# A mixture-of-experts step on one core: another order of the three kinds of expert pass

## The chip, the cores and the metric

The kernel runs on one core of a Trainium2 chip. The metric is device time in microseconds (us); lower is better. A core has TensorE (PE in the profile; its weight loads are listed as PEld), VectorE (DVE), ScalarE (ACT), GpSimd (POOL) and SyncE (SP). In this kernel SP issues nearly all transfers. Sixteen DMA engines carry them.

## The reference, cut to what matters

One layer of a decoder runs over 256 prompt tokens and 32 sample tokens, 288 tokens together, each 1024 wide. After attention and a state-space part, the last and by far the longest part is a mixture of 32 experts, in which each token uses 4:

```
logits = x2d @ w_router + b_router;  top_v, top_i = top_k(logits, 4);  gates = softmax(top_v)
h   = x_rows @ w_gate_up[e] + b_gate_up[e]              # 1024 -> 2048, for each expert e
act = min(h_even, 7) * sigmoid(1.702 * min(h_even, 7)) * (clip(h_odd, -7, 7) + 1)
out = act @ w_down[e] + b_down[e]                       # 1024 -> 1024
y[token] += gate * out                                  # summed over the token's four experts
```

All weights are float32: 8.4 MB of `w_gate_up` and 4.2 MB of `w_down` for each expert, 403 MB for all 32.

## The kernel before, in words

**Attention, state-space part and router** take up to about 190 us. The router counts how many tokens each expert has and sorts the experts by that count. Experts 0 and 1 always stand at positions 0 and 1.

**Kinds.** The experts run one after another at positions p = 0 to 31 (passes). `KINDS` gives each position one of three kinds. A narrow pass ("few") has room for 32 tokens, a medium pass ("mid") for 64, and a many-slot pass ("many") for 96: it does the work of a medium and of a narrow pass side by side. The sorted list fills the kinds: the fullest experts get the "many" positions, the next ones "mid", the emptiest "few" (`rank_at`, lines 1795 to 1803). There are 4 many, 14 mid and 14 few. Tokens that still don't fit would run in further passes behind position 31; this input has none.

**One pass on PE** (`expert`, line 1014): gate_up in eight chunks, one for every 128 of the 1024 input rows; the results of the pass before are combined in the middle of it (gates after chunk 1, `combine` after chunk 4). Then the hidden values are turned, the next pass's tokens are gathered and turned (`gather` for a wide pass, `gather_s` for a narrow one, both if the next is many), and `down` multiplies with `w_down`. ACT and DVE copy, clamp and gate between these steps, and DVE adds each pass's result to the output (`accumulate`, line 1925).

**Weights.** `gu_ring` has four slots of 2 MB, together one expert's `w_gate_up`. `dn_ring` has four, together two experts' `w_down`, in two halves each. SP (`load_others`, line 369) issues in the order dn(p), gu(p), dn(p+1), gu(p+1) and waits before each: gu(p) slot k waits until pass p-1 has used chunks 2k and 2k+1 (`gu_used`), and dn(p) half h waits until pass p-2 has used that half (`dn_used`). For the last pair the order is dn(30), gu(30), gu(31), dn(31). An expert is thus six transfers of 2 MB. All go through one queue in order.

**Loops.** On PE and ACT positions 0 and 1 are written out, positions 2 to 17 are a hardware loop of four rounds (`BODY`), positions 18 to 29 a loop of two rounds of six (`LATE`), and 30 and 31 are written out. On DVE only the four rounds are a loop; from position 18 on all is written out, with a few small operations between the passes that list the leftover tokens (`item_order`, `item_pass`).

Of the kernel before, what the change touches and what calls it, by code (L numbers as in the profile page):

```python
# [35 lines left out]
NE, TOPK = 32, 4  # L36
# [5 lines left out]
ITEMS = T * TOPK // SLOTS  # L42
PAIRS = NE // 2
GU_SLOTS = 4
GU_ROWS = KT // GU_SLOTS
FEW = 32
BODY, ROUNDS = ("few", "many", "few", "mid"), 4
LATE, LATER = ("few", "mid", "mid") * 2, 2
FIRST_LATE = 2 + len(BODY) * ROUNDS
KINDS = ["mid"] * 2 + list(BODY) * ROUNDS + list(LATE) * LATER + ["few"] * 2  # L50
ITEM_PART = 6
WIDE = [sum(k != "few" for k in KINDS[:p]) for p in range(NE + 1)]
SLIM = [sum(k != "mid" for k in KINDS[:p]) for p in range(NE + 1)]
# [24 lines left out]
def build(nc, a):  # L78
# [439 lines left out]
    def _(pe):  # L518
# [495 lines left out]
        def expert(p, w, s, kind, before, after, j, fill):  # L1014

            w_before, s_before = w - (before != "few"), s - (before != "mid")
            w_after, s_after = w + (kind != "few"), s + (kind != "mid")
            gate_up(p, w, s, kind, range(0, 2))
            if before == "bias":
                turn_gates(0)  # L1020
            else:
                if before == "many":
                    pe.wait_ge(S("ye_s_ready"), s_before + 1)
                if before != "few":
                    turn_gates(w)
                if before != "mid":
                    turn_gates_s(s_before)
            gate_up(p, w, s, kind, range(2, 5))
            if before == "bias":
                gate_bias()  # L1030
            else:
                combine(p, w_before, s_before, before)
            gate_up(p, w, s, kind, range(5, 8))
            pe.wait_ge(S("acc_done"), p * 4 + 4)
            if kind != "few":
                turn_hidden(w)
            if kind != "mid":
                turn_hidden_s(s)
            if after in ("mid", "many"):
                gather(w_after)  # L1040
            if after in ("few", "many"):
                gather_s(s_after)
            if after in ("mid", "many"):
                turn_gathered(w_after)
            if after in ("few", "many"):
                turn_gathered_s(s_after)
            if after is None:
                turn_gates_s(s)
            down(w, s, kind, after, s_after, j, fill)
# [4 lines left out]
        busy(0, xg[:, 0, 0:2 * P], 1)  # L1054
        expert(0, 0, 0, KINDS[0], "bias", KINDS[1], 0, 1)
        expert(1, 1, 0, KINDS[1], KINDS[0], KINDS[2], 1, 1)
        with pe.Fori(0, ROUNDS) as i:
            for k in range(4):
                expert(i * 4 + (2 + k), i * (WIDE[6] - WIDE[2]) + WIDE[2 + k], i * (SLIM[6] - SLIM[2]) + SLIM[2 + k],
                       BODY[k], BODY[k - 1], BODY[(k + 1) % 4], k % 2, i * 2 + (k // 2 + 2))  # L1060
        with pe.Fori(0, LATER) as i:
            for k in range(6):
                p = FIRST_LATE + k
                expert(i * 6 + p, i * (WIDE[p + 6] - WIDE[p]) + WIDE[p], i * (SLIM[p + 6] - SLIM[p]) + SLIM[p],
                       KINDS[p], KINDS[p - 1], KINDS[p + 1], k % 2, i * 3 + (p // 2 + 1))
        expert(NE - 2, N_WIDE, N_SLIM - 2, "few", "mid", "few", 0, PAIRS)
        expert(NE - 1, N_WIDE, N_SLIM - 1, "few", "few", None, 1, PAIRS)
        combine(NE, N_WIDE, N_SLIM - 1, "few")

        pe.wait_ge(S("list_ready"), 1)  # L1070
# [19 lines left out]
    def _(act):  # L1090
# [287 lines left out]
        def act_expert(p, w, s, kind, before, after):  # L1378

            w_after, s_after = w + (kind != "few"), s + (kind != "mid")  # L1380
            if before == "bias":
                act_gates(0)
            else:
                if before != "few":
                    act_gates(w)
                if before != "mid":
                    act_gates_s(s - 1)
            if kind != "few":
                act_gate(w)
# [12 lines left out]
            if after in ("mid", "many"):  # L1402
                act_turned(w_after)
            if after in ("few", "many"):
                act_turned_s(s_after)
            if after is None:
                act_gates_s(s)
            if kind != "few":
                act_result(p)
            if kind != "mid":  # L1410
                act_result_s(p)
# [2 lines left out]
        act_turned(0)  # L1414
        act_expert(0, 0, 0, KINDS[0], "bias", KINDS[1])
        act_expert(1, 1, 0, KINDS[1], KINDS[0], KINDS[2])
        with act.Fori(0, ROUNDS) as i:
            for k in range(4):
                act_expert(i * 4 + (2 + k), i * (WIDE[6] - WIDE[2]) + WIDE[2 + k], i * (SLIM[6] - SLIM[2]) + SLIM[2 + k],
                           BODY[k], BODY[k - 1], BODY[(k + 1) % 4])  # L1420
        with act.Fori(0, LATER) as i:
            for k in range(6):
                p = FIRST_LATE + k
                act_expert(i * 6 + p, i * (WIDE[p + 6] - WIDE[p]) + WIDE[p], i * (SLIM[p + 6] - SLIM[p]) + SLIM[p],
                           KINDS[p], KINDS[p - 1], KINDS[p + 1])
        act_expert(NE - 2, N_WIDE, N_SLIM - 2, "few", "mid", "few")
        act_expert(NE - 1, N_WIDE, N_SLIM - 1, "few", "few", None)

        act.wait_ge(S("list_ready"), 1)
        n = act.alloc_register("act_items")  # L1430
# [14 lines left out]
    def _(dve):  # L1445
        X = nc.vector
# [485 lines left out]
        def slots_of(c):  # L1932

            return pos[M, :, bass.ds(c, 1)]
# [55 lines left out]
        def expert_at(k, p):  # L1990
            dve.reg_load(regs[k], ord_e[0:1, p:p + 1] if isinstance(p, int) else ord_e[0:1, bass.ds(p, 1)])
            return dve.snap(regs[k], min_val=0, max_val=NE - 1)

        def expert(p, w, s, kind, before, after, x):

            x_before, x_now, x_after = x
            w_after, s_after = w + (kind != "few"), s + (kind != "mid")
            if before != "bias":
                if before != "few":
                    gated(slots_of(x_before), bass.ds(x_before, 1), w)  # L2000
                if before != "mid":
# [11 lines left out]
        dve.wait_ge(S("order_ready"), 1)  # L2013
        expert(0, 0, 0, KINDS[0], "bias", KINDS[1], (0, 0, 1))
        expert(1, 1, 0, KINDS[1], KINDS[0], KINDS[2], (0, 1, expert_at(0, 2)))
        with dve.Fori(0, ROUNDS) as i:
            x = [expert_at(k, i * 4 + (1 + k)) for k in range(6)]
            for k in range(4):
                expert(i * 4 + (2 + k), i * (WIDE[6] - WIDE[2]) + WIDE[2 + k], i * (SLIM[6] - SLIM[2]) + SLIM[2 + k],
                       BODY[k], BODY[k - 1], BODY[(k + 1) % 4], x[k:k + 3])  # L2020

        def expert_alone(p):
            expert(p, WIDE[p], SLIM[p], KINDS[p], KINDS[p - 1], KINDS[p + 1], [expert_at(k, p - 1 + k) for k in range(3)])

        expert_alone(18)
        expert_alone(19)
        item_order()
        for p in range(20, 26):
            expert_alone(p)
            item_pass(p - 20)  # L2030
        X.tensor_copy(list_e[:, 0:ITEMS + 1], list_f[:, 0:ITEMS + 1]).then_inc(S("list_ready"), 1)
        for p in range(26, NE - 1):
            expert_alone(p)

        n = dve.alloc_register("dve_items")
        x_reg = dve.alloc_register("dve_expert")
        y_reg = dve.alloc_register("dve_next")
        dve.wait_ge(S("list_ready"), 1)
        x_before, x_last = expert_at(0, NE - 2), expert_at(1, NE - 1)
        gated_s(slots_of(x_before), 0, bass.ds(x_before, 1))  # L2040
        accumulate(NE - 1)
        gated_s(slots_of(x_last), 0, bass.ds(x_last, 1))
        hidden_s(N_SLIM - 1, N_WIDE + N_SLIM - 1, x_last)
# [155 lines left out]
```

## Time and profile before

| | before |
|---|---|
| median of 3 runs | 1131.55 us (1131.29 to 1132.45) |
| profiled execution | 1130.87 us |
| its span | 1128.6 us |
| mean granted TensorE clock | 0.971 |
| PE busy | 987.5 us, 88% |
| DVE busy, ACT busy | 397.1 us, 35%; 205.1 us, 18% |
| bytes read from HBM | 419.86 MB |
| DMA over the span | 378 GB/s |

The times of all rows below count from the start of the span; 2.3 us of the profiled execution lie outside it. A matmul's end is modelled, and matmuls overlap a little, so where a step ends is best read from the start of the next one. An expert's pass is found in the rows by the tiles: `gu_ring,xe` is gate_up of a medium pass, `gu_ring,xe_s` of a narrow one, and `dn_ring,hT` and `dn_ring,hT_s` are their `down`. Where both tiles alternate, it is a many pass.

### The profile page before, as it was taken

Reading aid. Unit: us, or ns where it says so; the run is one execution under the profiler, and the core shown is the slowest. Engines: PE = TensorE matmul, PEld = TensorE weight load, DVE = VectorE, ACT = ScalarE, POOL = GpSimd, SP = SyncE. Lnnn points to the kernel's source line nnn. Section 1 sums busy time; section 2 is a strip of 40 time slices with the busy share of each in tenths; the row PEclk is TensorE's granted clock in tenths of the full one; section 3 lists DMA queues with packets and bytes.
Section 4 is the critical chain, followed back from the end, with each engine's and each line's share of the span. In section 5 each row is a group of like instructions: output and inputs, shape, how many; then the busy total and the mean of one; then the engine's idle time right before and its main releaser. Section 6 shows DMA issues by size and latency. Waiting matters only on the chain.

```text
span 1128.6 us, 16526 instructions
## 1 busy us (share of the span) xinstructions
PE 987.5 (88%) x6588; PEld 425.3 (38%) x6588; DVE 397.1 (35%) x898; ACT 205.1 (18%) x441; POOL 7.0 (1%) x7
## 2 busy tenths in 40 slices
PE   6987999999988898889988998979879878969985
PEld 5765875333233323322333233323333323323331
DVE  6978646222322222221323122313333333222223
ACT  4676333111111111110111111111111111111110
POOL 1000000000000000000000000000000000000000
PEclk9967999999999999999999999999999999999998
DMA  9513872899999999999999999999999999999995
GB/s 359 173 48 98 329 309 82 349 428 427 393 408 424 426 428 405 431 425 427 408 427 427 427 406 428 427 427 427 428 427 427 425 429 428 427 427 427 428 427 235
DMA packets 39149, 426.27 MB, mean 378 GB/s; under 512 B 7045, under 2 KB 10245, under 8 KB 12705
## 3 DMA queue, kind: packets, MB, share of 16 engines
q1 hardware_dynamic: 37296, 422.87, 89.6%
q10 hardware_dynamic: 1728, 2.11, 0.5%
q8 instruction: 63, 1.03, 0.4%
q0 software_dynamic: 48, 0.15, 0.0%
q14 instruction: 14, 0.11, 0.0%
HBM read 419.86 MB, written 2.51 MB: 374 GB/s over the span
## 4 chain that ended last, share of the span: by engine, by line
PE 70%; DMA 17%; DVE 6%; issue 3%; ACT 3%; ACTq 1%; DVEq 0%; SPq 0%
PE banks L520 66%; DMA gu_ring<-w_gu_dram 14%; DVE xT L1929 2%; DMA dn_ring<-w_dn_dram 2%; PE banks L906 1%; DVE raw L1883 1%; PE banks L862 1%; DVE hl L1895 1%; DVE hT L1900 1%; ACT gath L1323 1%; PE banks L960 1%; ACT x_tok L1312 1%; PE banks L913 1%; ACT s_p L1224 0%; PE banks L656 0%
## 5 line engine op out<-in xcount | busy, mean ns | idle before, releaser
L520 PE MATMUL banks<-gu_ring,xe 128*64 128x512 f32 x1152 | 269.8, 610 | 16.5 <-DMA gu_ring<-w_gu_dram 16.2
L1929 DVE TENSOR_TENSOR xT<-xT,banks 128x576 f32<-128x576 f32 x132 | 93.8, 751 | 491.8 <-PE banks L520 491.7
L520 PE MATMUL banks<-gu_ring,xe_s 128*32 128x512 f32 x1152 | 143.0, 608 | 22.7 <-issue 11.5
L520 PEld LDWEIGHTS banks<-gu_ring,xe 128*64 128x64 f32 x1152 | 77.7, 139 | 178.2 <-issue 153.8
L520 PE MATMUL banks<-dn_ring,hT 128*64 128x512 f32 x576 | 129.3, 597 | 4.9 <-DVE hT L1900 4.9
L520 PE MATMUL banks<-dn_ring,hT_s 128*32 128x256 f32 x1152 | 70.3, 392 | 5.6 <-ACT xe_s L1357 3.2
L520 PEld LDWEIGHTS banks<-gu_ring,xe_s 128*32 128x32 f32 x1152 | 29.8, 110 | 109.4 <-issue 87.1
L520 PEld LDWEIGHTS banks<-dn_ring,hT 128*64 128x64 f32 x576 | 39.2, 137 | 79.4 <-issue 73.0
L520 PE MATMUL banks<-gT,ye 64*128 64x288 f32 x288 | 48.9, 454 | 10.9 <-DVE xT L1929 10.9
L1338 ACT ACTIVATE raw<-banks 128x512 f32<-128x512 f32 x18 | 10.8, 597 | 248.7 <-PE banks L520 248.7
L520 PEld LDWEIGHTS banks<-dn_ring,hT_s 128*32 128x32 f32 x1152 | 35.7, 112 | 40.2 <-issue 17.1
L520 PE MATMUL banks<-x_tok,oh 96*64 96x512 f32 x216 | 50.3, 601 | 0.0
L520 PE MATMUL banks<-gT_s,ye_s 32*128 32x288 f32 x288 | 27.6, 453 | 21.7 <-DVE xT L1929 21.1
L1883 DVE COPY raw<-banks 128x512 f32<-128x512 f32 x18 | 12.4, 692 | 87.3 <-PE banks L520 87.3
L520 PEld LDWEIGHTS banks<-gT,ye 64*128 64x128 f32 x288 | 24.5, 192 | 42.6 <-DVE xT L1929 24.5
L520 PE MATMUL banks<-xg,w_in 128*128 128x288 f32 x160 | 39.8, 406 | 0.0
L1367 ACT ACTIVATE raw_s<-banks 128x512 f32<-128x512 f32 x18 | 10.8, 597 | 144.5 <-PE banks L520 144.5
L1347 ACT ACTIVATE ye<-banks 128x512 f32<-128x512 f32 x18 | 10.8, 597 | 135.9 <-PE banks L520 135.9
L520 PEld LDWEIGHTS banks<-xg,w_in 128*128 128x128 f32 x160 | 30.4, 190 | 8.4
L520 PE MATMUL banks<-aT,w_out 128*128 128x288 f32 x128 | 32.3, 409 | 1.0 <-ACT aT L1263 1.0
L906 PE MATMUL banks<-ident,raw 128*128 128x128 f32 x144 | 26.8, 309 | 2.2
L906 PEld LDWEIGHTS banks<-ident,raw 128*128 128x128 f32 x144 | 20.0, 208 | 20.3 <-issue 14.7
(347 smaller groups left out, 864.6 us busy)
## 6 DMA issues: line engine op xcount, KB each, us to landing
gu_ring<-w_gu_dram SPq DMA_DIRECT2D x120, 2048.0 KB, 19.9
dn_ring<-w_dn_dram SPq DMA_DIRECT2D x64, 2048.0 KB, 18.0
gu_ring<-w_gu_dram SPq DMA_DIRECT2D x16, 1024.0 KB, 8.3
w_out<-w_out_dram SPq DMA_DIRECT2D x2, 2048.0 KB, 10.0
w_in<-w_in_dram SPq DMA_DIRECT2D x3, 1024.0 KB, 16.3
w_in<-w_in_dram SPq DMA_DIRECT2D x4, 512.0 KB, 9.9
W<-W1c SPq DMA_DIRECT2D x16, 128.0 KB, 2.3
w_glu<-w_glu_dram SPq DMA_DIRECT2D x1, 2048.0 KB, 8.6
```

Of the source, the lines that this page charges most:

```text
L520: return nc.tensor.matmul(out, lhsT, rhs, start=start, stop=stop, **kw)
L862: last = pe.transpose(pb[6][:, c * P:(c + 1) * P], gath[:, c * P:(c + 1) * P], ident[:])
L906: last = pe.transpose(pb[2 + part][:, c * P:(c + 1) * P], hidden_cols(raw[:, part], c), ident[:])
L913: last = pe.transpose(pb[0][:, c * P:(c + 1) * P], hidden_cols(raw_s[:], c), ident[:])
L960: last = pe.transpose(pb[7][:, t * MT:(t + 1) * MT], goh[0:MT, t], ident[0:MT, 0:MT])
L1312: A(half.rearrange("p (s i f) -> p s f i", i=GU_ROWS, f=P), pb[XB[u]][0:MT, :].rearrange("p (s f i) -> p s f i", i=GU_ROWS, f=P), ACT.Copy ...
L1323: A(gath[:], pb[5][:], ACT.Copy).then_inc(S("gath_ready"), 1)
L1338: A(blocks_out(raw[:, 0]), blocks_in(pb[0]), ACT.Copy).then_inc(S("g_copied"), 1)
L1883: X.tensor_copy(blocks_out(raw[:, 1]), blocks_in(pb[1])).then_inc(S("l_copied"), 1)
L1895: X.scalar_tensor_tensor(out=hl[:], in0=hl[:], scalar=1.0, in1=hg[:], op0=ALU.add, op1=ALU.mult).then_inc(S("h_step"), 1)
L1900: X.scalar_tensor_tensor(out=hT[:], in0=th[:], scalar=1.0, in1=hl[:], op0=ALU.add, op1=ALU.mult).then_inc(S("h_ready"), 1)
L1929: X.tensor_tensor(two, two, pair[(1, 3)[n % 2]].rearrange("p (h f) -> p h f", h=2)[:, :, 0:T], ALU.add).then_inc(S("acc_done"), 1)
```

## The change

The order of kinds is another. The number of each kind stays the same.

```
position   0 1 | 2 ...                                              31
before     M M | f X f M  f X f M  f X f M  f X f M | f M M f M M f M M f M M | f f
after      M M f | f X M f  f X M f  f X M f  f X M f | f M M f M M f M M f M M | f
           M = medium, f = narrow (few), X = many-slot
```

So each round of four becomes narrow, many, medium, narrow, and starts one position later. The last four positions were medium, medium, narrow, narrow and become narrow, medium, medium, narrow. On PE and ACT the late part is no longer a loop. The order in which SP issues the loads is untouched.

```diff
-BODY, ROUNDS = ("few", "many", "few", "mid"), 4
-LATE, LATER = ("few", "mid", "mid") * 2, 2
-FIRST_LATE = 2 + len(BODY) * ROUNDS
-KINDS = ["mid"] * 2 + list(BODY) * ROUNDS + list(LATE) * LATER + ["few"] * 2
+BODY, ROUNDS = ("few", "many", "mid", "few"), 4
+FIRST_ROUND = 3
+FIRST_LATE = FIRST_ROUND + len(BODY) * ROUNDS
+KINDS = ["mid"] * 2 + ["few"] + list(BODY) * ROUNDS + ["few", "mid", "mid"] * 4 + ["few"]
...
+        def expert_alone(p):
+            expert(p, WIDE[p], SLIM[p], KINDS[p], KINDS[p - 1], KINDS[p + 1] if p + 1 < NE else None, p % 2, p // 2 + 1)
+
+        expert_alone(2)
         with pe.Fori(0, ROUNDS) as i:
             for k in range(4):
-                expert(i * 4 + (2 + k), i * (WIDE[6] - WIDE[2]) + WIDE[2 + k], i * (SLIM[6] - SLIM[2]) + SLIM[2 + k],
-                       BODY[k], BODY[k - 1], BODY[(k + 1) % 4], k % 2, i * 2 + (k // 2 + 2))
-        with pe.Fori(0, LATER) as i:
-            for k in range(6):
-                p = FIRST_LATE + k
...
+                p = FIRST_ROUND + k
+                expert(i * 4 + p, i * (WIDE[7] - WIDE[3]) + WIDE[p], i * (SLIM[7] - SLIM[3]) + SLIM[p],
+                       BODY[k], BODY[k - 1], BODY[(k + 1) % 4], p % 2, i * 2 + (p // 2 + 1))
+        for p in range(FIRST_LATE, NE):
+            expert_alone(p)
         combine(NE, N_WIDE, N_SLIM - 1, "few")
```

ACT is changed in the same way. DVE's loop moves by one position too, `item_order` stands behind position 20 instead of 19, the six `item_pass` behind 21 to 26 instead of 20 to 25, and at the end DVE prepares the gates of a medium pass 30 (`gated`) instead of a narrow one (`gated_s`). `rank_at` is written in pieces of evenly spaced positions: the narrow positions took three pieces and now take six, the others as many as before.

## Rows read from the trace of the kernel before

**Rows 1.** Windows: us; busy of PE, PEld, DVE, ACT, POOL; PEclk, DMA share, GB/s

```profile
225.00:680.00 455.00, 408.13 (x3093) 145.67 (x3091) 117.84 (x260) 53.53 (x115) 0.00 (x0) 1.00 0.99 420
680.00:1110.00 430.00, 368.36 (x2356) 134.03 (x2357) 129.27 (x254) 46.32 (x91) 0.00 (x0) 0.98 1.01 427
```

**Rows 2.** Chain that ended last, at its end: start, us, what

```profile
1090.54 26.09 DMA dn_ring<-w_dn_dram
...
1116.66 2.81 PE banks L520 x32
```

**Rows 3.** Timeline of PE, positions 7 to 10: start, us, engine, line, operation

```profile
391.12 1.94 PE L520 MATMUL banks<-gu_ring,xe 128*64 128x512 f32 x8
...
419.43 1.50 PE L520 MATMUL banks<-x_tok,oh_s 96*32 96x256 f32 x24
...
422.05 3.65 PE L520 MATMUL banks<-dn_ring,hT 128*64 128x512 f32 x16 [0.17 <-DVE hT L1900]
...
433.12 1.90 PE L520 MATMUL banks<-gu_ring,xe_s 128*32 128x512 f32 x16
...
447.86 2.79 PE L520 MATMUL banks<-x_tok,oh 96*64 96x512 f32 x12
...
451.94 3.66 PE L520 MATMUL banks<-dn_ring,hT_s 128*32 128x256 f32 x64
455.53 3.65 PE L520 MATMUL banks<-gu_ring,xe 128*64 128x512 f32 x16
...
477.84 7.09 PE L520 MATMUL banks<-dn_ring,hT 128*64 128x512 f32 x32 [0.41 <-DVE hT L1900]
487.06 1.92 PE L520 MATMUL banks<-gu_ring,xe_s 128*32 128x512 f32 x16 [2.13 <-issue]
```

**Rows 4.** Timeline of SP's queue: issues of w_down for positions 9, 11, 13

```profile
429.77 4.06 SPq L343 DMA_DIRECT2D dn_ring<-w_dn_dram  x2
481.67 3.76 SPq L343 DMA_DIRECT2D dn_ring<-w_dn_dram  x2
549.00 4.06 SPq L343 DMA_DIRECT2D dn_ring<-w_dn_dram  x2
```

**Rows 5.** Issue to landing: gu(4) slot 0 (277.6), dn(5) (310.2), dn(19) (720.1)

```profile
DMA to landing us min/median/max: 18.0/18.0/18.0
...
DMA to landing us min/median/max: 7.8/7.8/7.8
...
DMA to landing us min/median/max: 16.6/16.6/16.6
```

**Rows 6.** Timeline of PE, positions 18 and 29 to 31

```profile
723.33 1.92 PE L520 MATMUL banks<-gu_ring,xe_s 128*32 128x512 f32 x16
...
739.51 3.66 PE L520 MATMUL banks<-dn_ring,hT_s 128*32 128x256 f32 x64
...
1046.53 3.60 PE L520 MATMUL banks<-gu_ring,xe 128*64 128x512 f32 x16
...
1075.73 1.92 PE L520 MATMUL banks<-gu_ring,xe_s 128*32 128x512 f32 x16
...
1082.46 1.07 PE L520 MATMUL banks<-gu_ring,xe_s 128*32 128x512 f32 x8 [2.55 <-DMA gu_ring<-w_gu_dram]
...
1093.65 3.66 PE L520 MATMUL banks<-dn_ring,hT_s 128*32 128x256 f32 x64 [0.47 <-ACT xe_s L1357]
...
1097.12 1.90 PE L520 MATMUL banks<-gu_ring,xe_s 128*32 128x512 f32 x16
...
1102.12 1.07 PE L520 MATMUL banks<-gu_ring,xe_s 128*32 128x512 f32 x8 [0.84 <-DMA gu_ring<-w_gu_dram]
...
1112.75 3.64 PE L520 MATMUL banks<-dn_ring,hT_s 128*32 128x256 f32 x32 [2.11 <-DVE hT_s L1922]
```

**Rows 7.** Timeline of DVE: the copies that write rank_at

```profile
161.08 0.71 DVE L1801 COPY place<-iota 128x4 f32<-128x4 f32 x9
```

More of the change, by code:

```diff
@@ L1056, in _ @@
         expert(1, 1, 0, KINDS[1], KINDS[0], KINDS[2], 1, 1)
+        def expert_alone(p):
+            expert(p, WIDE[p], SLIM[p], KINDS[p], KINDS[p - 1], KINDS[p + 1] if p + 1 < NE else None, p % 2, p // 2 + 1)
+        expert_alone(2)
         with pe.Fori(0, ROUNDS) as i:
             for k in range(4):
-                expert(i * 4 + (2 + k), i * (WIDE[6] - WIDE[2]) + WIDE[2 + k], i * (SLIM[6] - SLIM[2]) + SLIM[2 + k],
-                       BODY[k], BODY[k - 1], BODY[(k + 1) % 4], k % 2, i * 2 + (k // 2 + 2))
-        with pe.Fori(0, LATER) as i:
-            for k in range(6):
-                p = FIRST_LATE + k
[L1064 to L1067, printed above, removed]
+                p = FIRST_ROUND + k
[3 more added lines that the diff above has]
+            expert_alone(p)
         combine(NE, N_WIDE, N_SLIM - 1, "few")
@@ L1416, in _, with act_expert_alone @@
         act_expert(1, 1, 0, KINDS[1], KINDS[0], KINDS[2])
+        def act_expert_alone(p):
+            act_expert(p, WIDE[p], SLIM[p], KINDS[p], KINDS[p - 1], KINDS[p + 1] if p + 1 < NE else None)
+        act_expert_alone(2)
         with act.Fori(0, ROUNDS) as i:
             for k in range(4):
-                act_expert(i * 4 + (2 + k), i * (WIDE[6] - WIDE[2]) + WIDE[2 + k], i * (SLIM[6] - SLIM[2]) + SLIM[2 + k],
+                p = FIRST_ROUND + k
+                act_expert(i * 4 + p, i * (WIDE[7] - WIDE[3]) + WIDE[p], i * (SLIM[7] - SLIM[3]) + SLIM[p],
                            BODY[k], BODY[k - 1], BODY[(k + 1) % 4])
[L1421 to L1427, printed above, removed]
+        for p in range(FIRST_LATE, NE):
+            act_expert_alone(p)
         act.wait_ge(S("list_ready"), 1)
@@ L2015, in _ @@
         expert(1, 1, 0, KINDS[1], KINDS[0], KINDS[2], (0, 1, expert_at(0, 2)))
[L2016 to L2020, printed above, removed]
         def expert_alone(p):
             expert(p, WIDE[p], SLIM[p], KINDS[p], KINDS[p - 1], KINDS[p + 1], [expert_at(k, p - 1 + k) for k in range(3)])
[L2025 to L2028, printed above, removed]
-            expert_alone(p)
[L2030 to L2033, printed above, removed]
+        expert_alone(2)
+        with dve.Fori(0, ROUNDS) as i:
+            x = [expert_at(k, i * 4 + (2 + k)) for k in range(6)]
+            for k in range(4):
+                p = FIRST_ROUND + k
+                expert(i * 4 + p, i * (WIDE[7] - WIDE[3]) + WIDE[p], i * (SLIM[7] - SLIM[3]) + SLIM[p],
+                       BODY[k], BODY[k - 1], BODY[(k + 1) % 4], x[k:k + 3])
+        for p in range(FIRST_LATE, NE - 1):
+            expert_alone(p)
+            if p == FIRST_LATE + 1:
+                item_order()
+            if FIRST_LATE + 1 < p < FIRST_LATE + 8:
+                item_pass(p - (FIRST_LATE + 2))
+            if p == FIRST_LATE + 7:
+                X.tensor_copy(list_e[:, 0:ITEMS + 1], list_f[:, 0:ITEMS + 1]).then_inc(S("list_ready"), 1)
         n = dve.alloc_register("dve_items")
@@ L2039, in _ @@
         x_before, x_last = expert_at(0, NE - 2), expert_at(1, NE - 1)
-        gated_s(slots_of(x_before), 0, bass.ds(x_before, 1))
+        gated(slots_of(x_before), bass.ds(x_before, 1), N_WIDE)
         accumulate(NE - 1)
```

## The prediction

> **What bounds the kernel now.** I read the rate of the transfers first, then the chain, then the timelines of PE and SP. From 680 to 1110 us the DMA engines move 427 GB/s with no gap (DMA share 1.01), while PE is busy for 368 of 430 us [rows 1]. A transfer of 2 MB (2097152 bytes) takes 4.9 us at that rate, and an expert, six of them, 29.5 us. So the late part is bound by the weights, and PE waits for them (2.55 us and 0.84 us in the last two passes) [rows 6]. From 225 to 680 us the rate is 420 GB/s [rows 1]: 455 us times 7/427 is 7.5 us in which the DMA engines had nothing to do. In that stretch PE is the longer one. Each round of four begins 119.2 us after the one before (549.00 - 429.77) [rows 4], against 4 x 29.5 = 118. At the end the chain waits 26.09 us for the last half of `w_down` and goes on with PE at 1116.66 [rows 2]. A change of order moves no byte. It can change three things: the DMA engines' idle time in the rounds, PE's time for a round, and what PE still has to do once the last weights have landed.
>
> **Lengths of the pieces of a pass, from [rows 3, 6].** "Front" is from the start of gate_up to the start of `down`.
> - Many, next narrow: front 422.05 - 391.12 = 30.9, `down` 433.12 - 422.05 = 11.1. The first half of `w_down` is released 429.77 - 422.05 = 7.7 after `down` began [rows 3, 4].
> - Narrow after many, next medium: front 451.94 - 433.12 = 18.8, `down` 3.6.
> - Narrow after medium, next medium: front 739.51 - 723.33 = 16.2. So to combine a many pass costs 2.6 more than a medium one.
> - Narrow after medium, next narrow: front 1093.65 - 1075.73, less the wait of 2.55, = 15.4, 0.8 shorter because less is gathered.
> - Medium after narrow: front 477.84 - 455.53 = 22.3, `down` 7.1, its first half released after 3.8 (481.67) [rows 3, 4].
> - The loop's back edge: 2.1 us of "issue" before 487.06. From there to the next many pass it is 391.12 + 119.2 - 487.06 = 23.3, which holds whatever the edge costs later.
>
> **Part 1, the many pass is followed by a medium one.** This pair is not in the trace. The medium pass's gather takes 2.79 us against 1.50 for the narrow one [rows 3], and in a many pass nothing is left that hides it. The front becomes longer by between 0 (all hidden behind DVE) and 2.8 (the whole gather late). I take the difference of the gathers, 1.3: front 32.2. The medium pass behind it has to combine the many pass: 22.3 + 2.6 = 24.9. With M the start of the many pass, the medium one starts at M + 32.2 + 11.1 = M + 43.3, its `down` at M + 68.2, and it releases its half of `w_down` at M + 72.0. A transfer issued into an empty queue lands 7.8 us later [rows 5], so at M + 79.8. If the queue never ran dry, this transfer, the 16th after the slot that started M, would land at M + 16 x 4.9 = M + 78.4. The queue therefore still runs dry for 1.4 us in each round, but behind the medium pass instead of within the many pass (its own release at M + 39.9 would land at M + 47.7, and 10 transfers take until M + 49.0). The Trainium skill, page "DMA: Bandwidth & Descriptors", section "Anatomy of one DMA", gives a fixed cost of about 2.0 us for a transfer beside its bytes. This trace shows 7.8 - 4.9 = 2.9 on a transfer of SP's queue, and the measured one stands. By 2.0 the sum would be lower by 0.9.
>
> **Part 2, PE's time for a round.** M + 68.2 + 7.1 (medium `down`) + 15.4 + 3.6 (narrow, next narrow) + 2.1 (edge) + 23.3 = M + 119.7. By the transfers it is 79.8 + 8 x 4.9 = M + 119.0. The two nearly coincide (4.9 us for each transfer is the bare rate), whereas before PE alone decided with a margin. Paths so close end a little after the later one, and I take 120.0, 0.8 more than before.
>
> **Part 3, the first round.** Positions 2 and 3 are both narrow now, so PE is at the first many pass early and waits for its weights: gu(4) slot 0 was issued at 277.6 and landed 18.0 later, at 295.6 [rows 5]. The fourth many pass then starts at 295.6 + 3 x 120.0 = 655.6. The transfer that follows the medium pass behind it is dn(19), which lands at 655.6 + 79.8 = 735.4; before it landed at 720.1 + 16.6 = 736.7 [rows 5]. From there to the end both orders are bound by the same 77 transfers. All that the new rounds do to the stream of weights is -1.3 us. The idle time that goes with the first many pass comes back as four small gaps and a slower round.
>
> **Part 4, the loop that goes.** The late part's back edge lies where PE waits for weights anyway (2.55 us in a late narrow pass [rows 6]). It is worth 0, and 2.1 if that cover were missing. The page "Runtime: NRT & Kernel Launch" of the Trainium skill, section "Instruction fetch mechanics", says that a taken branch breaks the sequential prefetch and that kernels therefore prefer unrolling. The 2.13 us at the edge agree. By that rule alone the change would give 2.1 us.
>
> **Part 5, the end.** Before, the last passes were medium, narrow, narrow, and PE was waiting when the last `w_down` landed. Now they are medium, medium, narrow. The second medium pass of a pair started at 1046.53 as position 29 [rows 6] and is now position 30, one expert of weights later: 1076.0. A medium pass after a medium one, next narrow, took 1075.73 - 1046.53 = 29.2 without a wait, so the last pass starts at 1105.2. Its front, 1112.75 - 1097.12 less the wait of 0.84 = 14.8, and a `down` of 3.6 end at 1123.6. The last weights still land at 1116.6. The gain of part 3 moves both ends alike. Before, `down` ended at 1116.66 + 2.81 = 1119.5 [rows 2]. PE now has the later end, by 4.1 us. What follows is the same: one narrow combine, four additions, the output. What would shorten this is only an earlier start of that medium pass, and its weights forbid it.
>
> **Part 6, three more small copies** for `rank_at`, nine in 0.71 us [rows 7], ahead of work on which the router waits: +0.2.
>
> **Sum:** 0.2 - 1.3 + 0 + 4.1 = +3.0. The profiled execution of 1130.87 (span 1128.6 and 2.3 around it) would be 1133.9. The median of the runs is 0.7 above that execution, so I predict 1134.6. The lower bound of part 1's front (0 instead of 1.3) takes 1.3 from each of three rounds and from the last release, 5.2 together, and makes the sum -2.2 or 1129.4. The upper one (2.8) adds 1.5 x 4 = 6.0 and makes it +9.0 or 1140.6. I stay near the middle, since the row of the gather is the nearest one.
>
> **Rivals.**
> - A, the end is covered: the last narrow pass finds its hidden values ready, the extra 4.1 does not appear and 0.2 - 1.3 = -1.1 is left: 1130.5. For it: DVE and ACT have slack. Against it: all of the 14.8 + 3.6 is PE's own chain with one wait for DVE. Chance 0.2.
> - B, the other side (against my forecast of slower): the rounds never let the queue run dry. Two narrow passes in a row give PE a lead just before the many pass, and if the medium pass's release comes before M + 70 the 7.5 us of idle time all go. Then 7.5 of the stream is won: 0.2 - 7.5 + 4.1 = -3.2, 1128.3. This needs a front shorter by 2 us than worked out and a PE round below 118. It decides from the point where the round falls under 118 us. Chance 0.13.
> - C, both late paths give way: the medium pass behind the many one releases 1.2 us later still (its gather waits for ACT, or PE's clock falls while it waits for weights before the many pass), and since no margin is left each of the four rounds carries it: 4 x 1.2 = 4.8 more, 1139.4. For it: before, PE had room to absorb such a thing, now both paths are critical. Chance 0.2.
> - My forecast: 0.47.
>
> The change does what it says: no token passes from one kind to another, as the counts of kinds are equal.
>
> **Numbers.** A measurement of this kernel tells 0.2%, 2.3 us, from no change: below 1129.3 is faster, above 1133.8 slower. Faster holds B, 0.13. Slower holds C and most of my forecast, which stands only 0.8 above the bound: 0.2 + 0.39 = 0.59. The rest, 0.28, is no change. The range reaches from 1129.5 (the lower bound, and A with a little from the stream) to 1139.5 (C). My case alone would be 1132.5 to 1137.
>
> **What would show it.** In the profile of the changed kernel: (1) the rate from 305 to 315 us near 427 GB/s, with dips near 365 to 375 and once a round after; (2) a period of 119.5 to 120.5 us; (3) many passes that start when their weights land, the first at about 295.6; (4) the last half of `w_down` landed near 1115 while PE is still in gate_up or before `down` of the last pass, which ends near 1122; (5) the chain at the end on PE, not on the DMA of `dn_ring`. If the last `down` still waits for `dn_ring`, part 5 is wrong. If the rate shows no dips in the rounds, part 1 is. If the period is over 121, C is right.

## The result, and the profile after

The changed kernel takes 1137.79 us (median of 15 runs, 1132.75 to 1144.24), the kernel before 1132.31 us (15 runs on the same chip, 1129.29 to 1135.46): a ratio of 1.0048, 95% interval 1.0034 to 1.0062. It is slower, by 5.5 us where 3.0 was predicted. On another chip the same kernel took 1136.54 us (12 runs) against 1133.64, 1.0023 [0.9999, 1.0046], an interval that just reaches no loss. So the loss is some 2.6 to 5.5 us. The profiled execution of the changed kernel took 1139.23 us, with a span of 1137.3 and a mean granted clock of 0.964.

The windows, which answer to [rows 1] (us; busy of PE, PEld, DVE, ACT, POOL; PEclk, DMA share, GB/s); the narrow ones are the idle times within a round:

```profile
225.00:680.00 455.00, 403.52 (x3043) 143.20 (x3045) 114.34 (x252) 51.69 (x111) 0.00 (x0) 0.97 0.99 417
305.00:315.00 10.00, 8.49 (x56) 2.35 (x54) 2.56 (x4) 0.00 (x0) 0.00 (x0) 0.96 1.02 433
365.00:380.00 15.00, 14.00 (x87) 4.78 (x89) 3.06 (x8) 1.55 (x4) 0.00 (x0) 1.00 0.94 376
485.00:500.00 15.00, 13.84 (x93) 4.48 (x85) 3.03 (x9) 2.29 (x5) 0.00 (x0) 1.00 0.93 371
680.00:1110.00 430.00, 374.10 (x2347) 135.82 (x2340) 128.85 (x254) 47.28 (x93) 0.00 (x0) 0.97 1.00 426
```

The one window of these where the kernel before had its gap:

```profile
305.00:315.00 10.00, 10.00 (x102) 3.40 (x98) 1.24 (x5) 0.87 (x2) 0.00 (x0) 1.00 0.70 262
```

The large gap in the first many pass is gone (262 before, 433 after). Gaps have come behind the medium pass: 376 and 371 instead of 427 over 15 us, some 2 us of idle time in each round. And a smaller one is left in the many pass, at its own release of `w_down`, which now comes later (337.82, 458.67 and 581.22 in the first three rounds, 310.22 in the first before). The largest of these:

```profile
570.00:585.00 15.00, 14.30 (x114) 4.88 (x112) 5.53 (x17) 2.43 (x5) 0.00 (x0) 1.00 0.89 355
```

That is 2.5 us of idle time. Over the whole stretch the rate is no better (417 against 420), and the late part is the same.

PE's timeline through two rounds, which answers to [rows 3]:

```profile
296.07 1.94 PE L520 MATMUL banks<-gu_ring,xe 128*64 128x512 f32 x8 [0.49 <-DMA gu_ring<-w_gu_dram]
...
330.10 3.65 PE L520 MATMUL banks<-dn_ring,hT 128*64 128x512 f32 x16
...
341.28 3.65 PE L520 MATMUL banks<-gu_ring,xe 128*64 128x512 f32 x16
...
366.07 7.09 PE L520 MATMUL banks<-dn_ring,hT 128*64 128x512 f32 x32 [0.42 <-DVE hT L1900]
373.08 1.92 PE L520 MATMUL banks<-gu_ring,xe_s 128*32 128x512 f32 x16
...
388.25 3.66 PE L520 MATMUL banks<-dn_ring,hT_s 128*32 128x256 f32 x64 [0.55 <-ACT xe_s L1357]
391.72 1.91 PE L520 MATMUL banks<-gu_ring,xe_s 128*32 128x512 f32 x16
...
398.47 1.07 PE L520 MATMUL banks<-gu_ring,xe_s 128*32 128x512 f32 x8 [2.60 <-DMA gu_ring<-w_gu_dram]
...
418.55 1.94 PE L520 MATMUL banks<-gu_ring,xe 128*64 128x512 f32 x8
...
450.94 3.65 PE L520 MATMUL banks<-dn_ring,hT 128*64 128x512 f32 x16
...
541.10 1.94 PE L520 MATMUL banks<-gu_ring,xe 128*64 128x512 f32 x8
660.14 1.94 PE L520 MATMUL banks<-gu_ring,xe 128*64 128x512 f32 x8 [1.86 <-DMA gu_ring<-w_gu_dram]
```

SP's releases by the medium pass, once a round (they answer to [rows 4]):

```profile
369.90 3.76 SPq L343 DMA_DIRECT2D dn_ring<-w_dn_dram  x2
490.75 3.76 SPq L343 DMA_DIRECT2D dn_ring<-w_dn_dram  x2
613.29 3.76 SPq L343 DMA_DIRECT2D dn_ring<-w_dn_dram  x2
732.33 3.76 SPq L343 DMA_DIRECT2D dn_ring<-w_dn_dram  x2
```

Issue to landing of the first transfer of the first and fourth of these, and of the last two transfers of all (issued from 1097.0 to 1097.5), as in [rows 5]:

```profile
DMA to landing us min/median/max: 9.0/9.0/9.0
...
DMA to landing us min/median/max: 7.6/7.6/7.6
...
DMA to landing us min/median/max: 17.7/19.9/22.1
```

So the last weights are there at 1097.5 + 22.1 = 1119.6, 3.0 later than before. PE's last two passes, which answer to [rows 6], are not waiting for them:

```profile
1078.76 3.60 PE L520 MATMUL banks<-gu_ring,xe 128*64 128x512 f32 x16
...
1107.97 1.92 PE L520 MATMUL banks<-gu_ring,xe_s 128*32 128x512 f32 x16
...
1122.57 5.35 PE L520 MATMUL banks<-dn_ring,hT_s 128*32 128x256 f32 x64 [2.11 <-DVE hT_s L1922]
```

And the end of the chain (start, us, what) is PE's from well before that landing, where it was the transfer's in [rows 2]:

```profile
1089.60 6.74 PE banks L520 x32
...
1100.95 8.94 PE banks L520 x48
...
1110.29 3.42 PE banks L520 x28
...
1114.55 4.18 PE banks L520 x32
```

The span is 8.7 us longer than before (1137.3 - 1128.6): 3.0 because the last weights land later, 5.7 because the span ends 17.7 us after them instead of 12.0. The first part moves from one execution to the next (in the profile on the other chip they landed at 1115.2), the second does not (17.6 there).

### The profile page after: what moved, and what is told of

Read it like the earlier page. It is cut to its first block, busy times and chain, and to the rows that moved or that the text cites. A ratio compares the mean times of both kernels' runs of the same rounds, so it can differ in the third digit from the quotient of the medians.

```text
span 1137.3 us, 16455 instructions
## 1 busy us (share of the span) xinstructions
PE 995.4 (88%) x6588; PEld 426.0 (37%) x6588; DVE 396.7 (35%) x901; ACT 205.2 (18%) x441; POOL 7.0 (1%) x7
## 3 DMA queue, kind: packets, MB, share of 16 engines
q10 hardware_dynamic: 1728, 2.11, 0.5%
## 4 chain that ended last, share of the span: by engine, by line
PE 68%; DMA 19%; DVE 7%; ACT 3%; issue 2%; ACTq 1%; DVEq 0%; SPq 0%
PE banks L520 65%; DMA gu_ring<-w_gu_dram 19%; DVE xT L1929 2%; PE banks L906 1%; DVE raw L1883 1%; PE banks L862 1%; PE banks L960 1%; ACT gath L1323 1%; ACT x_tok L1312 1%; ACT s_p L1224 0%; DVE hl L1895 0%; DVE hT L1900 0%; PE banks L913 0%; PE banks L656 0%; PE banks L967 0%
## 5 line engine op out<-in xcount | busy, mean ns | idle before, releaser
L520 PE MATMUL banks<-gu_ring,xe 128*64 128x512 f32 x1152 | 275.1, 620 | 20.8 <-DMA gu_ring<-w_gu_dram 20.6
L520 PE MATMUL banks<-gu_ring,xe_s 128*32 128x512 f32 x1152 | 146.0, 618 | 17.1 <-DMA gu_ring<-w_gu_dram 17.0
L520 PE MATMUL banks<-gT_s,ye_s 32*128 32x288 f32 x288 | 30.5, 496 | 21.7 <-DVE xT L1929 21.1
L520 PEld LDWEIGHTS banks<-gT_s,ye_s 32*128 32x128 f32 x288 | 12.3, 200 | 45.2 <-DVE xT L1929 28.6
```

What stands on the lines that cost most here:

```text
L520: return nc.tensor.matmul(out, lhsT, rhs, start=start, stop=stop, **kw)
```

## The experiments

M is medium, f narrow, X many-slot. Times are medians in us, each beside the kernel before on the same chip.

| kernel | order | time (range, runs) | before | ratio [95%] |
|---|---|---|---|---|
| changed | MMf (fXMf)x4 (fMM)x4 f | 1137.79 (1132.75-1144.24, 15) | 1132.31 | 1.0048 [1.0034, 1.0062] |
| after_again | the same | 1136.54 (1131.8-1143.3, 12) | 1133.64 | 1.0023 [0.9999, 1.0046] |
| end_back | MMf (fXMf)x4 (fMM)x3 MMff | 1132.99 (1127.27-1137.12, 12) | 1133.28 | 0.9997 [0.998, 1.0013] |
| end_alone | MM (fXfM)x4 (fMM)x3 ffMMf | 1138.73 (1134.86-1143.62, 11) | 1133.28 | 1.0046 [1.0031, 1.0061] |
| unrolled | as before | 1131.55 (1129.99-1136.49, 12) | 1133.28 | 0.9987 [0.9971, 1.0002] |
| body_back | MMf (fXfM)x4 (fMM)x4 f | 1129.1 (1126.87-1130.32, 7) | 1133.28 | 0.9959 [0.9944, 0.9974] |
| no_loop | as before | 1127.91 (1126.08-1130.52, 6) | 1133.79 | 0.9952 [0.9935, 0.997] |
| both_back | MMf (fXfM)x4 (fMM)x3 MMff | 1124.12 (1123.76-1125.09, 5) | 1133.79 | 0.9917 [0.9903, 0.9931] |
| both_no_loop | the same | 1125.12 (1123.49-1125.36, 5) | 1133.79 | 0.9921 [0.9906, 0.9935] |
| end_warm | as changed | 1136.69 (1132.21-1141.53, 12) | 1133.79 | 1.0026 [1.0009, 1.0043] |
| rounds_warm | as changed | 1137.24 (1132.36-1140.74, 12) | 1133.64 | 1.0029 [1.0009, 1.005] |
| both_warm | as changed | 1134.2 (1131.68-1140.45, 12) | 1133.64 | 1.0012 [0.9992, 1.0032] |
| mid_first | MMf (fMXf)x4 (fMM)x4 f | 1134.81 (1131.93-1140.17, 12) | 1133.64 | 1.0007 [0.9988, 1.0026] |

### The end: put back, and made alone

**end_back**: the changed kernel with before's last four kinds. (Of each experiment only the lines that matter are shown. Here DVE also prepares the gates of pass 30 with `gated_s` again, as that pass is narrow.)

```diff
-KINDS = ["mid"] * 2 + ["few"] + list(BODY) * ROUNDS + ["few", "mid", "mid"] * 4 + ["few"]
+KINDS = ["mid"] * 2 + ["few"] + list(BODY) * ROUNDS + ["few", "mid", "mid"] * 3 + ["mid", "mid", "few", "few"]
```

> The changed kernel's rounds with an end of two narrow passes: positions 28 to 31 are medium, medium, narrow, narrow instead of narrow, medium, medium, narrow. Theory 'end' (a medium pass at position 30 leaves PE 4 to 5.5 us of work behind the last weights): this is 4 to 5.5 us faster than the changed kernel (1137.8), so 1132.3 to 1133.8, within 1.5 us of the kernel before. Theory 'rounds' (the medium pass behind each many pass and the clock that falls while PE waits before it cost the time): it keeps the loss, 1136 to 1138. In the profile, by 'end', the last down waits for dn_ring again and ends about 3 us after the last landing instead of 8.

**end_alone**: before's rounds, at before's positions, with a narrow pass last behind two medium ones.

```diff
-BODY, ROUNDS = ("few", "many", "mid", "few"), 4
-FIRST_ROUND = 3
+BODY, ROUNDS = ("few", "many", "few", "mid"), 4
+FIRST_ROUND = 2
-KINDS = ["mid"] * 2 + ["few"] + list(BODY) * ROUNDS + ["few", "mid", "mid"] * 4 + ["few"]
+KINDS = ["mid"] * 2 + list(BODY) * ROUNDS + ["few", "mid", "mid"] * 3 + ["few", "few", "mid", "mid", "few"]
```

> The rounds of the kernel before with the new end: positions 27 to 31 are narrow, narrow, medium, medium, narrow instead of narrow, medium, medium, narrow, narrow; the late part is written out. Theory 'end': 4 to 5.5 us slower than the kernel before (1132.3), 1136.3 to 1137.8. Theory 'rounds': no difference, 1132.

Measured: 0.9997 and 1.0046. With before's end the changed kernel is as fast as before. With the new end alone the kernel before loses 5.2 us. end_alone also has the late part written out, as the changed kernel has. Against unrolled (below), the kernel before with just that, it loses more, 6.7 us by the two ratios (1.0046 and 0.9987). The chain's end of end_back is that of [rows 2] again, the wait for `w_down` and then PE:

```profile
1090.02 26.15 DMA dn_ring<-w_dn_dram
...
1116.22 1.98 PE banks L520 x32
```

The whole measured loss is thus the end's (part 5), and rival A is refuted. The new rounds give nothing and cost nothing that can be measured (end_back is also 1.1 us above unrolled by the ratios, within their intervals).

### The loop edges

**unrolled**: before's order, with positions 18 to 31 written out on PE and ACT as in the changed kernel. **no_loop**: before's order, everything from position 2 written out, on DVE too. In outline, PE's part:

```diff
 # unrolled
+        with pe.Fori(0, ROUNDS) as i:      # positions 2 to 17, before's BODY
+        for p in range(FIRST_LATE, NE):    # instead of before's loop over LATE
+            expert_alone(p)
 # no_loop
-        with pe.Fori(0, ROUNDS) as i:
-            for k in range(4):
-                ...
-        for p in range(FIRST_LATE, NE):
+        for p in range(2, NE):
             expert_alone(p)
```

> The order of the kernel before, with only the late part on PE and ACT written out instead of a loop of two rounds of six. Both main theories: no difference (within 0.5 us), because PE waits for weights in that part. Rival 'fetch' (a taken branch stalls the engine and the written-out form wins that back): 2 us faster. Rival 'fetch the other way' (more code has to be brought in and the transfers share the queues): 1 to 2 us slower, which would be part of the change's loss.

> The order of the kernel before, with all passes from position 2 written out on PE, ACT and DVE, so that no loop edge is left. If the edge (2.1 us of issue and 1.5 more a few chunks later, three times in the rounds) holds up PE where PE is the longer one: a period of 119.2 falls to the transfers' 118, so about 1.2 x 3 = 3.6 us faster, 1129; the first gap of the many pass stays. Rival 'no edge cost' (code has to be brought in either way): 1132 to 1133. Writing out the late part alone gave 1131.6 against 1133.3.

Writing out the late part gives 1.5 us, with an interval from a gain of 3.3 to a loss of 0.2: it excludes neither the 0 of part 4 nor the 2.1 of its rule. All edges together give 5.4 us (interval 3.4 to 7.4). PE's timeline of no_loop shows that the 2.13 us of "issue" behind the medium pass [rows 3] are gone, 358.54 + 7.09 and on at once:

```profile
358.54 7.09 PE L517 MATMUL banks<-dn_ring,hT 128*64 128x512 f32 x32 [0.49 <-DVE hT L1885]
365.56 1.92 PE L517 MATMUL banks<-gu_ring,xe_s 128*32 128x512 f32 x16
```

In the rounds before, where PE was the longer path, the edge did cost time: the releases by the many pass (310.53, 428.63, 545.84, 664.80) come 118.1 us apart on average, which is the 4 x 29.5 of the transfers, where they were 119.2 apart before. The first gap stays (262 GB/s from 305 to 315 us). Its chain at the end shows the last weights 3 us earlier than in [rows 2]:

```profile
1087.47 26.11 DMA dn_ring<-w_dn_dram
...
1113.62 1.98 PE banks L517 x32
```

### The rounds: the same shift, without the many-medium pair

**body_back**: the changed kernel with before's order within a round (narrow, many, narrow, medium), still one position later. Its loop covers positions 7 to 18 in three rounds, and the first round is written out, on all three engines. So it has one edge fewer than the kernel before, beside the late part's.

```diff
-BODY, ROUNDS = ("few", "many", "mid", "few"), 4
-FIRST_ROUND = 3
+BODY, ROUNDS = ("few", "many", "few", "mid"), 3
+FIRST_ROUND = 7
-KINDS = ["mid"] * 2 + ["few"] + list(BODY) * ROUNDS + ["few", "mid", "mid"] * 4 + ["few"]
+KINDS = ["mid"] * 2 + ["few"] + list(BODY) * (ROUNDS + 1) + ["few", "mid", "mid"] * 4 + ["few"]
```

> The changed kernel with a narrow pass between the many and the medium pass again (order after position 2: narrow, many, narrow, medium, four times), the early narrow pass at position 2 and the new end kept. The loop on PE, ACT and DVE covers positions 7 to 18, three rounds instead of four, so one back edge fewer. Theory 'end' alone: equal to the changed kernel less what the stalls behind the medium passes cost, which my arithmetic puts at 5 to 6 us: 1130 to 1132.5, because the start of two narrow passes takes away the long gap of the first many pass. Theory 'rounds are neutral': 1137. In the profile the issue-to-landing gap at the medium pass's release is gone and the many passes start 2 to 5 us after their weights landed.

Measured 1129.1, 0.9959, although it still has the slow end. The window from 225 to 680 us and the end of its chain:

```profile
225.00:680.00 455.00, 408.57 (x3083) 143.94 (x3077) 115.02 (x252) 52.10 (x112) 0.00 (x0) 0.98 1.01 427
```

```profile
1113.05 5.39 PE banks L520 x64
```

The rate is 427, against 417 to 420 in both the kernel before and the changed one: here the queue hardly runs dry. Against the kernel before two things differ in the rounds, the narrow pass more ahead of the first many pass and the fewer loop edges, and this run does not separate them. That the narrow pass is a gain by itself is shown by no_loop and both_no_loop (below), which have no loop at all. Against the changed kernel, whose edges show no cost (part 2 below), what body_back gives back is the price of the medium pass right behind the many one. The chain still ends on PE, in the whole of the last `down` (x64) at the lower clock.

**mid_first**: the heavy pair turned round, medium before many.

```diff
-BODY, ROUNDS = ("few", "many", "mid", "few"), 4
+BODY, ROUNDS = ("few", "mid", "many", "few"), 4
```

> The changed kernel with the body narrow, medium, many, narrow instead of narrow, many, medium, narrow: the medium pass stands before the many pass. Theory 'two heavy passes in a row' (what costs is that PE falls behind the weights by two passes without a narrow one between, and the second of them releases w_down late): the same as the changed kernel within 1.5 us, 1136 to 1139, with the gap now behind the many pass. Rival 'the combine of the many pass in a medium pass' (its longer gates and combine, 2.6 us, are what makes the release late): most of the 9 to 10 us that a narrow pass behind the many pass gave back is won here too, 1129 to 1131.

Measured 1134.81, which is 1.7 below after_again on the same chip and not to be told from it. It lies between the two ranges of its expectation, below the 1136 to 1139 of 'two heavy passes' and well above the 1129 to 1131 of its rival. The queue now runs dry behind the many pass:

```profile
490.00:505.00 15.00, 15.00 (x146) 5.47 (x142) 0.63 (x3) 1.58 (x4) 0.00 (x0) 1.00 0.85 340
```

Its ratio of 1.0007 [0.9988, 1.0026] is apart from body_back's 0.9959 [0.9944, 0.9974]. So what costs is mainly that two heavy passes stand side by side, whichever is first.

### Both parts taken back: the faster kernel

**both_back**: body_back with before's last four kinds. It is the order of before with one narrow pass moved from position 27 to position 2, the late part and the first round written out. **both_no_loop**: the same order, all written out.

```diff
-KINDS = ["mid"] * 2 + ["few"] + list(BODY) * ROUNDS + ["few", "mid", "mid"] * 4 + ["few"]
+KINDS = ["mid"] * 2 + ["few"] + list(BODY) * (ROUNDS + 1) + ["few", "mid", "mid"] * 3 + ["mid", "mid", "few", "few"]
```

> Medium, medium, narrow, then narrow, many, narrow, medium four times, then narrow, medium, medium three times, medium, medium, narrow, narrow. Only the second narrow pass at position 2 and 3 is left of the change. If the end's cost and the rounds' cost are separate terms that add, this is the kernel with a narrow pass behind each many pass (1129.1) less the 5.4 us that the new end cost: 1123.5 to 1124.5, 8 to 9 us faster than the kernel before. Theory 'transfers only' (the earlier start only moves the idle time, and the end hides it): 1129. In the profile the last w_down lands near 1110 and the last down ends 2 to 3 us later.

> The order of the run before this one in name ('both back'), with all passes from position 2 written out. If that order already keeps the transfers without a gap, the loop edges are covered and this gives nothing more: the same time within 1 us, near 1124. If edges still cost, 2 to 3 us less, 1121.

Measured 1124.12, 9.4 us below the kernel before, and 1125.12. Two windows and the end of the chain of both_back:

```profile
225.00:680.00 455.00, 406.65 (x3105) 145.06 (x3105) 117.25 (x256) 52.70 (x113) 0.00 (x0) 0.99 1.01 427
680.00:1105.00 425.00, 370.10 (x2363) 135.41 (x2351) 132.10 (x264) 47.81 (x95) 0.00 (x0) 0.98 1.01 427
```

```profile
1083.76 25.43 DMA dn_ring<-w_dn_dram
...
1109.24 3.69 PE banks L520 x32
```

The stream runs at one rate from 225 us to its end, and the last weights are on the chain 7.4 us earlier than in [rows 2]. The end counts here as it does in end_back: body_back to both_back is 0.9959 to 0.9917, 4.8 us. Writing out the loops that are left adds nothing, as the edges lie beside a stream that is the bound everywhere.

How much of the 9.4 us is the order's? both_no_loop and no_loop, on the same chip, have no loop in either and differ only in where the one narrow pass stands: 1125.12 (1123.49 to 1125.36) against 1127.91 (1126.08 to 1130.52), 2.8 us, or 3.5 by the ratios. Writing out everything in before's order gives 5.4. The move alone, with before's loops kept, was not run. It may be worth more than 3.5 there, since it also covers the edges that are left.

### The clock

In the changed kernel PE waits for weights in the narrow pass ahead of a many one, and its granted clock is low there (windows as above):

```profile
395.00:410.00 15.00, 10.16 (x67) 3.00 (x58) 3.50 (x6) 0.60 (x1) 0.00 (x0) 0.77 1.01 430
515.00:530.00 15.00, 10.51 (x64) 2.47 (x64) 2.84 (x4) 0.32 (x1) 0.00 (x0) 0.66 1.00 428
```

The kernel before had 1.00 from 395 to 410. Three kernels keep PE at work with products whose result nobody reads. **end_warm** puts them ahead of the last `down`, **rounds_warm** into each narrow pass before a many one, **both_warm** does both.

```diff
 # rounds_warm, in expert
+            if kind == "few" and after == "many":
+                gate_up(p, w, s, kind, range(2, 4))
+                busy(1, ident[:], 10)
+                gate_up(p, w, s, kind, range(4, 5))
+            else:
                 gate_up(p, w, s, kind, range(2, 5))
 # end_warm, behind the turning of the last pass's gates
+                busy(1, ident[:], 10)
```

> The changed kernel with ten further matmuls of 128 columns (their result is used by nothing) on PE while it waits for the hidden values of the last pass, just before its down. In the changed kernel's profile that down took 5.35 us against 3.66 for the same work at the full clock. If the wait of 2.1 us is what let the clock fall there: 1 to 1.7 us faster than the changed kernel, 1136 to 1137, down back at 3.7 us. Rival (the clock fell for what lay further back, as the wait for weights at the many passes does): no change, and down stays above 5 us in the profile.

> The changed kernel with ten further matmuls of 128 columns (used by nothing) on PE in each narrow pass that stands before a many pass, at the point where it waits 2.6 to 3 us for the third slot of gu_ring. In the changed kernel's profile the clock falls there (399 to 407 us, 519 to 530 us), the narrow pass and once the many pass become 2 to 3.3 us longer, and the period of the rounds is 120.9, 122.5 and 119.0 us. Theory 'clock' (that fall costs the rounds their time, because behind it nothing is in reserve): periods near 119.3, 3 to 5 us faster than the changed kernel (1137.8), so 1133 to 1135, and a smaller spread than its 11 us. Rival 'release' (the late release of w_down behind the medium pass sets the pace whatever the clock does): 0 to 1 us, 1137.

> The changed kernel with both sets of further matmuls, in the narrow pass before each many pass and before the last down. If the clock's two places are separate terms: 5 to 7 us faster than the changed kernel, 1131 to 1133, which would be what the order itself costs without the clock, about the time of the kernel before. Rival: no more than the better of the two alone, 1135.

PE at the end of end_warm, the filler and the last `down`:

```profile
1119.44 2.42 PE L520 MATMUL banks<-ident 128*128 128x128 f32 x20
1121.79 3.66 PE L520 MATMUL banks<-dn_ring,hT_s 128*32 128x256 f32 x64
```

The `down` is back at 3.66 us, 1.7 shorter than the 5.35 of the changed kernel, where PE had stood idle for 2.11 us ahead of it. The granted clock was 1.00 from 1121 to 1126 us here, and 0.66 from 1122 to 1125.5 in the changed kernel. That piece of the tail is the clock's. But the filler isn't needed for it, and the wait alone does not decide it. These are the same `down` in rounds_warm (no filler at the end), in end_alone, and its first half in both_no_loop:

```profile
1122.88 3.66 PE L520 MATMUL banks<-dn_ring,hT_s 128*32 128x256 f32 x64 [2.10 <-DVE hT_s L1927]
```

```profile
1125.63 6.59 PE L520 MATMUL banks<-dn_ring,hT_s 128*32 128x256 f32 x64 [2.11 <-DVE hT_s L1920]
```

```profile
1107.04 1.93 PE L517 MATMUL banks<-dn_ring,hT_s 128*32 128x256 f32 x32 [2.26 <-DVE hT_s L1907]
```

Behind the same wait the 64 products take 3.66, 5.35 or 6.59 us. From the start of this `down` to the end of the span it is 13.0 us in rounds_warm and end_warm, 14.7 in the changed kernel and 15.8 in end_alone, so the profiles do show the time. end_warm, with one profile, doesn't show that its filler held the clock. What decides it was not tried. The ratios differ by less than their intervals (1.0026 against 1.0048 and 1.0023), so the runs' times don't show the 1.7.

The same places in rounds_warm (windows 5 us longer), with the clock held:

```profile
395.00:415.00 20.00, 17.25 (x149) 7.19 (x141) 5.88 (x14) 3.35 (x8) 0.00 (x0) 1.00 1.01 431
515.00:535.00 20.00, 17.77 (x175) 7.69 (x163) 7.12 (x19) 2.40 (x5) 0.00 (x0) 1.00 1.01 430
```

Here PE waits for weights at the start of the last three many passes (1.85, 0.97 and 0.84 us). In the changed kernel's profile it waits, of these three, only at the fourth, and the third starts late, behind a narrow pass at the lower clock. The periods are 121.9, 119.2 and 119.0 us, against 120.9, 122.5 and 119.0 there and 121.5, 119.1 and 119.1 in after_again. Two of the three are thus near the 119.3 of the theory 'clock'. But its time is no better than that of after_again (1.0029 against 1.0023), and its transfer behind the fourth medium pass is issued at 732.72, as late as in the changed kernel (732.33). So the lower clock in the rounds can cost one execution a little and is not what makes the runs long.

both_warm gave 1134.2, 1.0012 [0.9992, 1.0032]: 2.3 below after_again, which the intervals don't separate, and above the 1131 to 1133 of two terms that add.

**after_again**: the changed kernel once more, beside the last kernels.

> The changed kernel once more, beside the others on the same chip: 1137 to 1138, 5 to 5.5 us slower than the kernel before, with a spread of 8 to 11 us between its executions.

Measured 1136.54, a loss of 2.6 us by the ratio, half of the 5 to 5.5 expected. Its last `down` takes the same 5.35 us:

```profile
1118.13 5.35 PE L520 MATMUL banks<-dn_ring,hT_s 128*32 128x256 f32 x64 [2.10 <-DVE hT_s L1922]
```

## Why the prediction was right, and where it was not

The sign, the place and the mechanism were right: the change loses at the end, on PE, and the rounds give nearly nothing. The measured 1137.79 lies 3.2 above the predicted 1134.6, inside the range, near its slow end. The two profiles show both cases that were named: 1134.87 lies in my own case (1132.5 to 1137), 1139.23 beside rival C's 1139.4. Point by point, with the sum's own terms:

- **Part 1, many then medium: right in the main.** Front of the many pass 450.94 - 418.55 = 32.4 (predicted 32.2; the first one, at 34.0, was longer, with eight products in it that took 3.32 us instead of 1.94). Medium front 366.07 - 341.28 = 24.8 (24.9), its release 3.8 after `down` began. The gap appeared behind the medium pass as worked out. It did not only move, though: one of up to 2.5 us was left in the many pass, since the first many pass had the longer front and the second and third started later than their weights landed (part 2). The size behind the medium pass was a little low: two of the four transfers landed 9.0 and 9.5 us after issue instead of 7.8, two 7.6, so the gap is between 1.2 (1.4 - 0.2) and 3.1 us (1.4 + 1.7).
- **Part 2, PE's round: its edge did not appear.** The sum had 2.1 of "issue" between the two narrow passes and 1.5 more within its 23.3. In the trace `down` at 388.25 + 3.66 is followed by gate_up at 391.72, and instead PE waits for weights 2.60 us later. The edge's cost was read from a medium-narrow pair, and behind a narrow pass it isn't visible. Where PE keeps its clock, the round is therefore set by the medium pass's release and the eight transfers: 613.29 + 7.6 + 8 x 4.9 = 660.1, and the fourth many pass starts at 660.14 after a wait. The second and third start without a wait, 0.5 and 1.6 us after their weights by the same sum (369.90 + 9.0 + 39.2, 490.75 + 9.5 + 39.2), behind narrow passes with a granted clock of 0.77 and 0.66. The period, from release to release, still came out near the 120.0 taken: 120.9, 122.5 and 119.0, mean 120.8, and 119.9 in the second profile. Right in size, in part for a wrong reason, and that part is luck: an edge that wasn't there stood for slower landings and a slower clock.
- **Part 3, the rounds' net: -1.3 predicted.** The first many pass started at 296.07 (295.6). The transfer behind the fourth medium pass landed at 732.33 + 7.6 = 739.9, not at 735.4: 0.5 from the start, 1.8 from the first release (73.8 after M, not 72.0), 2.4 from three periods, less 0.2. In the second profile it landed at 735.5, as predicted. Taken over runs the net is 0 (end_back, 0.9997, an interval of -2.3 to +1.5 us). The -1.3 lies inside that and is neither shown nor refuted.
- **Part 4, the late loop:** 0 predicted, 1.5 measured (-0.2 to 3.3), open. What that part left out is that the edge in the rounds before was not covered: no_loop gives 5.4, all edges together. The Trainium skill, page "Runtime: NRT & Kernel Launch", section "Instruction fetch mechanics", prefers unrolling. The runs agree where PE is the longer path (no_loop) and not where the stream is (both_no_loop, 1.0 slower than both_back, not to be told apart).
- **Part 5, the end: the term that was mis-sized.** +4.1 predicted, 5.7 in both profiles, 4.8 to 5.2 in runs (body_back against both_back, end_alone), and 6.7 for end_alone against unrolled. The pass lengths were right: 1107.97 - 1078.76 = 29.2 (29.2), front 1122.57 - 1107.97 = 14.6 (14.8). The `down` was wrong, 5.35 instead of 3.6, and that is the 1.7 between 4.1 and 5.7. The row for it had been there: in the last row of [rows 6], behind the same wait of 2.11 us, 32 products take 3.64 us, as long as 64 take at 1093.65. I took 3.6 as the price of the whole `down`. Before, the slow half was hidden by the wait for the last weights. Now nothing hides it. It isn't a fixed cost: rounds_warm has 3.66 behind the same wait, end_alone 6.59.
- **Part 6:** 12 copies in 0.94 us where 9 took 0.71: +0.2, as predicted.
- **Rival B** (the queue never runs dry) is wrong for this order and right for another: with a narrow pass behind the many one and the rounds one position later, the rate is the 427 that it asks for. **Rival C** (period over 121): from release to release the mean is 120.8, but from start to start of the many passes (296.07, 418.55, 541.10, 660.14) it is 121.4, over its bound, and one of its two reasons, PE's clock falling before the many pass, is in the trace. The transfer behind the fourth medium pass was 4.5 late, near C's 4.8. In the second profile (295.95 to 655.66) the mean is 119.9 and C does not hold. So C describes some executions, and rounds_warm says that its reason from the clock is not the whole of it.

Open: the changed kernel's runs spread over 11.5 us, those of after_again over 11.5, while both_back's spread over 1.3. Orders whose stream has no gap (body_back, both_back, both_no_loop) spread over 1.3 to 3.5 us, in 5 to 7 runs each; the others, in mostly more runs, over 4 to 12. rounds_warm, with the clock held where it had fallen, spread over 8 us all the same. The cause wasn't found. What the record shows is that the slower executions of the changed kernel are those with the lower mean granted clock (1132.75 us at 0.974, 1144.24 at 0.957). Which of the two brings the other isn't shown.

## What to carry to other kernels

In a kernel bound by a stream of weights, ask what the compute engine still has to do when the last transfer lands: light passes belong there, and a heavy one before the last moves the end of the chain from the transfer to the engine. A pass that releases late should have light ones on both sides: with them the rate here was 427 GB/s throughout; price the gap by the issue to landing of an isolated transfer, and look for it behind the next pass after it has gone from where it was. And try the parts of such a change one by one: here the shift by one position, with before's order in the rounds and before's end, made the kernel 0.8% faster, together with some loops written out (0.3% for the shift when no loop is left in either order), while the whole change lost 0.2 to 0.5%. Keep the loops the same in such a comparison, or run the loop's share by itself.

## What the runs showed of the hardware that was not expected

- The loop's back edge costs PE 2.13 us of "issue" behind a medium pass and nothing visible between two narrow ones (391.72 follows 388.25 + 3.66). Why it depends on the pass was not tried.
- A transfer of 2 MB into a queue that has just run dry landed after 9.0 and 9.5 us in two cases, 7.6 in two others, with 7.8 before, and in after_again after 9.0 once and 7.6 to 7.7 three times. Of that 4.9 are its bytes at 427 GB/s. The Trainium skill, page "DMA: Bandwidth & Descriptors", section "Anatomy of one DMA", has about 2.0 us beside the bytes, fitted to transfers that GpSimd issues. These are SyncE's. The trace has 2.7 to 4.6, and the measurement decides.
- Behind the same wait of 2.1 us the last `down` of 64 products took 3.66 us in one profile (rounds_warm), 5.35 in four (the changed kernel, after_again, body_back, mid_first), and 6.59 in another (end_alone). With products of 2.42 us put into the wait it took 3.66 in both profiles (end_warm, both_warm). So a wait of this length is followed by the lower clock in some kernels and not in others.
